# Linear attention's outputs one column later, its queries for the states made beside the masks, and the normalisation of the output two columns later

## The reference

```python
def step(s, inp):
    qq, kk, vv, aa = inp
    b = jnp.cumsum(aa, axis=2)
    b_last = b[:, :, -1:, :]
    s_new = jnp.exp(b_last)[:, :, 0, :, None] * s + einsum(kk * jnp.exp(b_last - b), vv)
    inter = einsum(qq * jnp.exp(b), s)           # the queries' states' part
    intra = attn(qq, kk, decay, masked) @ vv     # the masked part
    return s_new, inter + intra

y_gla = rmsnorm(o_forward + flip(o_backward), g) * silu(z['gla_gate'])
merged = g_mla * (y_mla @ w_bm) + g_pool * (y_pool @ w_bp) + g_gla * (y_gla @ w_bg)
out = merged @ w_out
```

## Time and profile before

| | |
|---|---|
| median of 3 runs | 1644.01 us (1642.89 to 1644.77) |
| the profiled execution's own time | 1642.83 us |
| its span | 1641.0 us |
| PE busy | 1507.7 us (92%) |
| DVE busy | 955.1 us (58%) |
| ACT busy | 770.3 us (47%) |
| share of PE in the chain that ended last | 76% |
| mean granted TensorE clock | 0.963 |

### The profile page before, as it was taken

How to read it: one execution, slowest core, us unless ns; L and a number is a source line. 1 busy time by engine, 2 the same in 40 slices (tenths; PEclk the granted TensorE clock), 3 DMA queues, 4 the chain that set the end, 5 groups by cost and what they waited for, 6 DMA issues and landing times.

```text
span 1641.0 us, 23866 instructions
## 1 busy us (share of the span) xinstructions
PE 1507.7 (92%) x9902; PEld 1308.2 (80%) x9902; DVE 955.1 (58%) x1522; ACT 770.3 (47%) x1212; POOL 125.8 (8%) x145
## 2 busy tenths in 40 slices
PE   6899999899999998999989886888999988889997
PEld 4767776787877775677988786877999988889997
DVE  5546875345453646576366557666566448767642
ACT  6534444432325354544535544565444358644342
POOL 0000000000000021000000013002122020122200
PEclk9999999899999999999999998999999999999999
DMA  9123333222222252322334454423666544446651
GB/s 369 64 64 116 128 103 116 77 78 77 77 77 96 84 181 85 97 90 69 99 121 137 154 185 154 131 77 103 207 192 186 187 142 142 141 149 186 193 182 63
DMA packets 58266, 212.57 MB, mean 130 GB/s; under 512 B 6384, under 2 KB 7536, under 8 KB 58032
## 3 DMA queue, kind: packets, MB, share of 16 engines
q1 hardware_dynamic: 56832, 205.29, 38.1%
q0 software_dynamic: 1328, 5.77, 1.1%
HBM read 209.98 MB, written 1.05 MB: 129 GB/s over the span
## 4 chain that ended last, share of the span: by engine, by line
PE 76%; DVE 13%; ACT 6%; DMA 3%; issue 1%; POOL 0%; SPq 0%; DVEq 0%; ACTq 0%; POOLq 0%
PE B L596 49%; PE B L612 7%; PE B L1005 7%; DVE WL L1785 4%; DMA RAW<-wstream 3%; PE B L719 3%; ACT WH L1200 3%; PE B L988 1%; PE B L1016 1%; PE B L799 1%; DVE M L2223 1%; PE B L786 1%; DVE X L2230 1%; PE B L621 1%; PE B L916 1%
## 5 line engine op out<-in xcount | busy, mean ns | idle before, releaser
L1785 DVE TENSOR_TENSOR WL<-RAW,WH 128x1024 fp32r<-128x1024 f32 x384 | 471.0, 1235 | 446.5 <-ACT WH L1200 445.5
L596 PE MATMUL B<-XH,WH 128*128 128x256 f32 (+1 forms) x1632 | 520.9, 319 | 11.4 <-ACT Z L1267 5.3
L596 PE MATMUL B<-XL,WH 128*128 128x256 f32 (+1 forms) x1632 | 505.7, 310 | 0.0
L596 PE MATMUL B<-XH,WL 128*128 128x256 f32 (+1 forms) x1632 | 505.6, 310 | 0.0
L1200 ACT ACTIVATE WH<-RAW 128x1024 fp32r<-128x1024 f32 x384 | 396.3, 1052 | 143.7 <-DMA RAW<-wstream 143.3
L596 PEld LDWEIGHTS B<-XH,WH 128*128 128x128 f32 x1632 | 313.5, 192 | 46.7 <-issue 16.6
L596 PEld LDWEIGHTS B<-XL,WH 128*128 128x128 f32 x1632 | 313.4, 192 | 20.3 <-issue 4.5
L596 PEld LDWEIGHTS B<-XH,WL 128*128 128x128 f32 x1632 | 313.1, 192 | 17.1
L612 PE MATMUL B<-XH,WH 128*128 128x256 f32 (+1 forms) x208 | 74.0, 356 | 39.5 <-DVE XL L2235 27.0
L1005 PE MATMUL B<-HH,WL 128*128 128x256 f32 x304 | 85.1, 280 | 0.0
L1005 PE MATMUL B<-HL,WH 128*128 128x256 f32 x304 | 85.1, 280 | 0.0
(11 more groups left out here) (320 smaller groups left out, 2539.3 us busy)
## 6 DMA issues: line engine op xcount, KB each, us to landing
RAW<-wstream SPq DMA_DIRECT2D x384, 512.0 KB, 3.5
X<-x_t SPq DMA_DIRECT2D x1, 2048.0 KB, 18.5
SW<-small POOLq DMA_DIRECT2D x2, 896.0 KB, 10.7
SW<-small POOLq DMA_DIRECT2D x2, 768.0 KB, 9.1
BT<-rel POOLq DMA_DIRECT2D x1, 1024.0 KB, 16.3
X<-consts POOLq DMA_DIRECT2D x1, 768.0 KB, 9.2
out_t<-X SPq DMA_DIRECT2D x3, 256.0 KB, 2.5
C<-consts SPq DMA_DIRECT2D x1, 624.0 KB, 14.1
```

The source lines that it names most:

```text
L596: last = mm(out, w, x, start=i == 0, stop=i == len(pairs) - 1)
L1785: v.tensor_tensor(lo_of(h), raw_of(h), hi_of(h).bitcast(f32), ALU.subtract).then_inc(lo_ready, 1)
```

## The change

Five things are moved, none is added or removed. PE makes a unit's outputs one step later (f = 7, 13, 19, 25 in place of 6, 12, 18, 24). ACT's squares and copies move with them (13 and 25 in place of 12 and 24). DVE's QE moves from step 6u + 1 to step 6u + 4, ahead of the masks, and its wait with it. The sums of squares, and ACT's logarithms, exponential and two table loads, move from step 26 to 28, DVE's `normed_output` from 28 to 30, ACT's `upper_branch(2)` from 30 to 31. The two slots that hold VG and the masked scores may be filled after 26 halves of the merge in place of 25; no slot of any half is another.

```diff
-OPENED = ((7, AT["merge", 0] + END, AT["merge", 0] + 25), (17, AT["merge", 0] + END, AT["merge", 0] + 25),
+OPENED = ((7, AT["merge", 0] + END, AT["merge", 0] + 26), (17, AT["merge", 0] + END, AT["merge", 0] + 26),
...
-          (10, AT["merge", 1] + END, AT["merge", 1] + 25), (17, AT["merge", 1] + END, AT["merge", 1] + 25),
+          (10, AT["merge", 1] + END, AT["merge", 1] + 26), (17, AT["merge", 1] + END, AT["merge", 1] + 26),
...
-                    if f % 6 == 0 and 6 <= f <= 24:
+                    if f % 6 == 1 and 7 <= f <= 25:
                         attended(f // 6 - 1)
-                    if f == 26:
+                    if f == 28:
                         output_sums()
...
-                    if f in (12, 24):
+                    if f in (13, 25):
                         j = f // 12 - 1
                         act.wait_ge(go_ready, 4 * l + 2 * j + 2)
...
-                    if f == 26:
+                    if f == 28:
                         tables(LN_EXP)
...
-                    if f == 30:
+                    if f == 31:
                         upper_branch(2)
...
                     v.tensor_tensor(KD[:, :], E1[:, :], k, ALU.mult).then_inc(kd_ready, 1)
+
+                def masked(u):
+                    d, j = unit_of(u)
                     if u > 0:
                         dve.wait_ge(go_ready, 4 * l + u)
-                    v.scalar_tensor_tensor(out=QE[:, t], in0=LG[:, r, t], scalar=GDK ** -0.5, in1=q, op0=ALU.mult, op1=ALU.mult)
-
-                def masked(u):
-                    d, j = unit_of(u)
+                    v.scalar_tensor_tensor(out=QE[:, t], in0=LG[:, 2 * d + j, t], scalar=GDK ** -0.5, in1=Z[:, Z_GQ + j, t],
+                                           op0=ALU.mult, op1=ALU.mult)
...
-                    if f == 28:
+                    if f == 30:
                         normed_output()
```

## The result

The changed kernel takes 1649.63 us (median of 12 runs, 1644.88 to 1658.14) against 1644.32 us of the kernel before in the same comparison (12 runs, 1641.97 to 1649.15). The ratio is 1.003, with a 95% interval of 1.0015 to 1.0044: slower by 4.9 us by the ratio and by 5.3 between the two medians, where 4.6 were forecast (1648.6). The profiled execution took 1649.69 us, its span is 1647.9 us.

A forecast was written before the change was run, and what follows sets the result against it. PE carries most of the chain, so only its waits in the two merges count. First layer +1.5, second layer +1.4 and clock +1.7 gave +4.6 us, added to 1644.0: 1648.6; range 1643.5 to 1652.0.

The forecast's parts named there:

- The outputs one column later: Second layer: two ST waits go, but PE then waits for KD; gain 0.2 us, bounds 0 and 1.9.
- The squares: Second layer, unit 2: squares and copies go behind the WH, KD comes 1.09 us earlier; gain 1.1, bounds 0 and 1.2.
- QE at nothing: Moving QE ahead of the masks on DVE costs nothing; bound 3.8 us in all if its cover were gone.
- First layer's sums: Sums of squares at step 28: a second WH lengthens PE's wait from 1.9 to 2.85; cost 0.95 us.
- Its tail: First layer: scaling and gating start at step 30, so PE waits at the end of step 31; cost 0.55 us.
- Second layer's sums: Half 28's slot opens a column later, ACT's list follows without a gap; PE waits 5.3 us where it waited 3.9.
- Third branch: Second layer's tail: y is ready after PE ends steps 29 to 31; wait 2.7 us (before 1.7), cost 2.7.
- The clock: Waits of 2.85 and 2.75 us may bring the clock down; one stretch charged, 1.7 us, bounds 0 and 3.4.
- the forecast with none: Rival: the same steps without a clock stretch, +2.9 us, 1646.9, counted as no change; chance 0.17.
- with both: Rival: the same steps with both stretches of low clock, +6.3 us, 1650.3, slower; chance 0.25.
- The rival of a burst landing out of order: Second layer: first of five halves issued at once lands after 6.1 us, not 3.4; +7.3, 1651.3; chance 0.05.
- The rival of whole gains: Both merges: tails stay hidden, gains at ST and KD are whole; -2.05 us, 1642.0, decided at KD's end; chance 0.13.

The follow-up runs named there:

- the one with three edits: Kernel before, with first pair's squares at step 13, table load, logarithms and exponential ahead of step 26's WH, and YL in step 30: 0.9988 (0.9975 to 1.0).

## Why the prediction was right

Its steps in its own order.

The outputs one column later, +0 to -1.9, taken as -0.2: right in kind. The two ST waits went and two KD waits of 1.1 came, one each at units 1 and 3, where 0.7 to 0.9 were named, so this part gave nothing at all: 1.9 went and 2.2 came. The rows for it were the slacks at KD.

The squares, -1.1: the wait of 1.2 us at unit 2 went, also in the kernel with this edit alone. In time it could not be shown; in the profile it comes out once a stretch of low clock is set aside.

QE at nothing: the kernel with QE alone has the bank waits of before, and 0.5 us more in two other waits.

First layer's sums, +0.95: measured 2.9 against 1.9, +1.0. Its tail, +0.55: 0.7.

Second layer's sums: a wait of 5.3 was forecast, 5.6 measured, and the reason (half 28 a column later, four WH, three tanh and four squares and copies ahead of the logarithm) is shown from two sides. With the last outputs, squares and slots as before the wait is 3.3; with two WH out of the way it is 3.8. Third branch: 2.7 forecast, 3.0 measured. On the way two sizes were off against each other: the column behind the sums took 4.06 us, 1.2 more than at full rate where 1.75 was charged, so step 28 ended 18.3 us after the start of the count and not 18.7; and PE stood before the third branch 0.6 us sooner than forecast (26.6 against 27.2) while y came 0.4 sooner (29.6 against 29.95).

The clock, +1.7 for one stretch of two possible: the profiled execution has both, and a third at the bank wait of 2.3 us in step 23, which the profile before doesn't have. Against that, the rest of the program took 1.3 us less than its share: from the start of the projection (965.91 after, 957.67 before, 8.2 apart) to the end the two spans (1647.9 and 1641.0, 6.9 apart) came closer again, where the clock at the projection's start (0.86 against 0.66) alone gives back 1.7. So the profiled execution is 6.9 slower than that of before, and the medians 5.3.

The sum, then. Without the clock 2.9 were forecast, and the wait rows grew by 3.8: the missing 0.9 is in the units' part, where 1.3 of gain was forecast and 0.9 came, and in waits that are each 0.1 to 0.3 longer than forecast. Of the 5.3 between the medians that leaves 1.5 for the clock, against 1.7 charged; the mean clocks, set out in the last section, give an estimate of 0.7 to 1.2. So the waits and their causes were right, and that the total came within a microsecond is partly luck: how many stretches an execution gets was a guess between none and two. The times can't decide it either, since the interval, 2.5 to 7.2 us, holds the forecast with none (2.9), with one (4.6) and with both (6.3). How many such stretches an execution gets differs between executions of one kernel: the runs of one comparison spread from 1644.88 to 1658.14, and their mean granted clock from 0.966 to 0.954. This is what the page of the Trainium skill, TensorE: Matmul & The Clock Gate, section What's actually happening, says of an observation that isn't tied to the program; the wait of 2.3 us in step 23, which is the same in both profiles and lowered the clock only in the one, agrees, and so does the kernel with QE alone, where the clock fell at it too.

The rival of a burst landing out of order fell: the first half landed 3.50 us after its issue, with one more half behind it. The rival of whole gains fell at KD, where it was said to be decided.

## What to carry to other kernels

A wait that is taken from the busiest engine only pays up to the next thing that engine needs; look up how much slack that has (here 0.1 us) before the gain is counted. When work that frees a buffer is moved later, follow the buffer: the transfer into it came a column later, PE never waited for the transfer, but ACT did, and all that ACT had to do for PE stood behind. A short answer on which the busiest engine waits (here a table load and a logarithm) belongs ahead of the work in bulk on its engine, and then the bulk has to be followed to the next queue.

## What the runs showed of the hardware

Waits of 1.9 to 2.3 us fell on either side of lowering TensorE's clock, in different executions and places: 1.9 at step 23 of the first layer lowered it before the change and with it, and not in the kernel with the last outputs left early; 2.3 in the second layer did not before, and did after. One such stretch costs 1.7 us, which is more than any single wait that these edits removed from the kernel before (1.2 at most). So with ten to twelve runs each, edits that take away a wait of 1 us, seen plainly in the wait rows, can't be told from no change in the times (0.9988 to 1.0005).

The granted clock of each execution takes most of this spread away. Within the executions of one kernel, a mean granted clock lower by 0.001 goes with a time longer by about 1.2 us (the changed kernel: 0.966 at 1644.88, 0.954 at 1658.14; its own slope is 1.1, those of the other kernels lie between 0.8 and 1.4). As an estimate, by that slope: the kernel with QE alone, whose mean time is 1.3 us lower than before (1642.6 against 1644.0), owes all of it to its clock; the one with three edits, whose mean time is 3.0 lower (1640.2 against 1643.2), gains 3 us or a little more at equal clock, near the 3.5 of its profile. The changed kernel's mean clock, 0.9611, is 0.0006 to 0.001 below that of the kernel before in the later comparisons (0.9617 to 0.9621), which is 0.7 to 1.2 us.
